# Layer ends of a four-layer block on one core: closing and opening in four and four pieces by token halves, with parts made ahead in idle buffers

## The reference

```python
def reference(x, ...):
    # layer 0: stick-breaking attention and a grouped state-space mixer
    h = rms_norm(x, g);  proj = h @ even_w_in          # 1024 x 5120
    x = x + concat([o_a, o_b]) @ even_w_out            # 1536 x 1024
    # layer 1: gated linear attention
    h = rms_norm(x, g);  proj = h @ odd_w_in           # 1024 x 3088
    x = x + (o * silu(z)) @ odd_w_out                  # 1024 x 1024
    # layers 2, 3: dilated window attention and retention
    for l in range(2):
        shift, scale, gate = split(silu(c) @ w_ada[l] + b_ada[l], 3)
        h = rmsnorm(x, norm_w[l]) * (1 + scale) + shift
        proj = h @ w_in[l]                             # 1024 x 11776
        merged = sigmoid(ga) * (y_att @ w_proj_attn[l]) + sigmoid(gr) * (y_ret @ w_proj_ret[l])
        x = x + gate * (merged @ w_out[l])
    return rmsnorm(x, final_norm_w)
```

## Time and profile before

| | |
|---|---|
| median of 3 runs | 1069.9 us (1068.21 to 1071.53) |
| the profiled execution | 1071.09 us |
| its span from first to last instruction | 1069.3 us |
| mean granted clock of TensorE | 0.986 |
| busy: TensorE, VectorE, ScalarE, GpSimd | 1019.7, 709.5, 566.0, 201.0 us |
| loads: read from HBM | 189.59 MB |

### The profile page before, as it was taken

The page is one execution under the profiler, slowest core; times in us unless marked ns, Lnnn a source line. Parts: engine busy times, 40 slices in busy tenths (PEclk is TensorE's granted clock), DMA queues, the critical chain, the costliest instruction groups (busy, mean ns, idle before and its releaser), DMA issues.

```text
span 1069.3 us, 15213 instructions
## 1 busy us (share of the span) xinstructions
PE 1019.7 (95%) x6020; PEld 894.4 (84%) x6020; DVE 709.5 (66%) x1111; ACT 566.0 (53%) x873; POOL 201.0 (19%) x212
## 2 busy tenths in 40 slices
PE   5899999979999899999999999989999999999995
PEld 5688889868977679998899888867999888998884
DVE  7884946988868656775566586664444555767666
ACT  6969567647435655445553344555444555334552
POOL 4700070433421100000004100020465000320001
PEclk9999999999999999999999999989999999999998
DMA  7543443958754658874466455545777446645551
GB/s 241 158 128 91 144 128 103 321 180 276 249 175 148 202 177 296 301 249 118 138 183 176 155 155 181 178 136 163 235 237 223 119 118 179 187 146 153 183 177 59
DMA packets 93046, 191.62 MB, mean 179 GB/s; under 512 B 6272, under 2 KB 9600, under 8 KB 92976
## 3 DMA queue, kind: packets, MB, share of 16 engines
q1 hardware_dynamic: 88560, 177.30, 53.7%
q0 software_dynamic: 3264, 10.65, 3.0%
q10 hardware_dynamic: 1152, 2.72, 0.7%
HBM read 189.59 MB, written 1.05 MB: 178 GB/s over the span
## 4 chain that ended last, share of the span: by engine, by line
PE 86%; DVE 8%; ACT 4%; issue 1%; DMA 1%; DVEq 0%; ACTq 0%
PE G L598 15%; PE G L600 14%; PE G L599 14%; PE G L607 8%; PE G L610 8%; PE G L609 8%; DVE WL L1521 2%; PE B L561 2%; ACT AR L1040 1%; ACT WH L1040 1%; DVE AR L1911 1%; PE G L636 1%; PE G L638 1%; PE G L637 1%; PE B L900 1%
## 5 line engine op out<-in xcount | busy, mean ns | idle before, releaser
L1521 DVE TENSOR_TENSOR WL<-RAW,WH 128x1024 fp32r<-128x1024 f32 (+2 forms) x306 | 383.3, 1255 | 251.7 <-ACT WH L1040 250.6
L1040 ACT ACTIVATE WH<-RAW 128x1024 fp32r<-128x1024 f32 (+2 forms) x306 | 320.2, 1049 | 282.5 <-PE G L600 144.9
L598 PE MATMUL G<-WH,HTh 128*128 128x512 f32 (+1 forms) x564 | 230.0, 408 | 7.3 <-DVE WL L1521 6.9
L607 PE MATMUL G<-HTh,WH 128*128 128x256 f32 x768 | 219.3, 286 | 0.5 <-DVE HTl L1597 0.5
L600 PE MATMUL G<-WL,HTh 128*128 128x512 f32 (+1 forms) x564 | 219.7, 389 | 0.0
L599 PE MATMUL G<-WH,HTl 128*128 128x512 f32 (+1 forms) x564 | 219.0, 388 | 0.0
L609 PE MATMUL G<-HTl,WH 128*128 128x256 f32 x768 | 217.8, 284 | 0.0
L610 PE MATMUL G<-HTh,WL 128*128 128x256 f32 x768 | 217.7, 283 | 0.0
L607 PEld LDWEIGHTS G<-HTh,WH 128*128 128x128 f32 x768 | 147.6, 192 | 1.9 <-issue 1.7
L609 PEld LDWEIGHTS G<-HTl,WH 128*128 128x128 f32 x768 | 147.6, 192 | 0.4 <-issue 0.2
L610 PEld LDWEIGHTS G<-HTh,WL 128*128 128x128 f32 x768 | 147.5, 192 | 0.0
(11 more groups left out here) (343 smaller groups left out, 1325.4 us busy)
## 6 DMA issues: line engine op xcount, KB each, us to landing
RAW<-in_w_in SPq DMA_DIRECT2D x176, 512.0 KB, 3.8
RAW<-in_even_w_in SPq DMA_DIRECT2D x40, 512.0 KB, 3.6
AR<-in_w_ada_t SPq DMA_DIRECT2D x32, 512.0 KB, 4.8
AR<-in_w_ada_g POOLq DMA_DIRECT2D x32, 256.0 KB, 4.0
RAW<-in_odd_w_in SPq DMA_DIRECT2D x16, 512.0 KB, 4.3
RAW<-in_w_proj_ret SPq DMA_DIRECT2D x16, 512.0 KB, 3.6
RAW<-in_w_out SPq DMA_DIRECT2D x16, 512.0 KB, 3.5
RAW<-in_even_w_out SPq DMA_DIRECT2D x12, 512.0 KB, 4.6
```

What stands on the lines that cost most here:

```text
L598: nc.tensor.matmul(o, xh, wh, start=begins, stop=False)
L607: nc.tensor.matmul(o, fh, h_[:, kx, :], start=begins and f % 2 == 0, stop=False, skip_group_check=True)
L1040: return nc.scalar.activation(out_, ps, ACT.Copy, **kw)
L1521: vt(wl, raw, wh.bitcast(F32), ALU.subtract).then_inc(*dve.mark(LO, n))
```

## The change

The closing has four pieces (CLOSE), the former lone piece among them, and the opening four (OPEN), each by token halves. The last half of a closing is run after the first eight transposes of the opening. Of each layer end six pieces (the closing's last three, the opening's first three) are not split into the rings but into places of the arena `AR` that are free by then (STAND; `ARR` is the same memory in the rounded type); the table `made` queues two splits each at times 2c - 5, 2c - 3 and 2c - 1, where c is the closing's first piece, and none in the six odd times after. ScalarE waits, before it splits into the arena, for the transposes and products that read those places. `next_layer` gets a new order on both engines, with the splits of the opening's third, fourth and fifth piece in it (fourth and fifth in the ring). The root loses two of its small steps: its first guess comes straight from -v/2. ScalarE scales columns 512 to 1023 in place of GpSimd, in the start too; in layers 2 and 3 VectorE makes the affine step of quarters 2 and 3. GpSimd's load of the reset mask moves behind the next load and waits for the opening's third piece. In the last layer only the closing's last three pieces stand in the arena.

```diff
 AHEAD = 2
+CLOSE, OPEN = 4, 4
 EPS = 1e-6
 NEG = -1e30
 MAGIC = 1597463007.0
+MAGIC_H = MAGIC - 2.0 ** 30 - 2.0 ** 22
 RND = 12582912.0
 C1 = 6.28125
...
@@ -321 @@
             v = w.rearrange("(c p) n -> p c n", p=P)
             groups["close", l] = dict(into=into, at=len(pieces), n=512)
-            for j, k in ((0, ks[1]), (1, ks[0]), (1, ks[1])):
+            for j, k in ((0, ks[0]), (0, ks[1]), (1, ks[0]), (1, ks[1])):
                 pieces.append(dict(src=v[:, k:k + KP, 512 * j:512 * j + 512], n=512, kind="C", group=("close", l), k=k,
                                    lhs=lhs, into=into[j], first=False, last=False, split=len(pieces) - groups["close", l]["at"]))
         def opening(name):
-            for i in range(3):
+            for i in range(OPEN):
                 pieces[groups[name]["at"] + i]["split"] = i
...
@@ -402 @@
         s_raw = [sem(f"raw{i}") for i in range(NRAW)]
         HI, LO = events("hi", range(NP)), events("lo", range(NP))
+        STAND = [[(9216, 10240), (11264, 12288)] + [(16896 + 2048 * i, 17920 + 2048 * i) for i in range(4)],
+                 [(4352, 5376), (6400, 7424)] + [(11776 + 2048 * i, 12800 + 2048 * i) for i in range(3)] + [(9728, 10752)],
+                 [(13568, 23424), (14592, 15616), (16640, 17664)] + [(7424 + 2048 * i, 8448 + 2048 * i) for i in range(3)],
+                 [(7424 + 2048 * i, 8448 + 2048 * i) for i in range(3)]]
+        held = {groups["close", l]["at"] + 1 + i: at for l, layer in enumerate(STAND) for i, at in enumerate(layer)}
+        ring = [n for n in range(NP) if n not in held]
+        slot = {n: i % NHL for i, n in enumerate(ring)}
+        before = {n: ring[i - NHL] for i, n in enumerate(ring) if i >= NHL}
+
+        def parts(n):
+
+            if n in held:
+                return tuple(ARR[:, at:at + KP * 512] for at in held[n])
+            return WH[:, slot[n], :], WL[:, slot[n], :]
+
         def w_in(n):
             w = KP * pieces[n]["n"]
-            return RAW[:, n % NRAW, 0:w], WH[:, n % NHL, 0:w], WL[:, n % NHL, 0:w]
+            return (RAW[:, n % NRAW, 0:w],) + tuple(x[:, 0:w] for x in parts(n))
+
+        made = {2 * n - 1: [n + AHEAD] for n in range(1, NP - AHEAD)}
+        for l in range(3):
+            c0 = groups["close", l]["at"]
+            made[2 * c0 - 5], made[2 * c0 - 3], made[2 * c0 - 1] = ([c0 + 2 * i, c0 + 2 * i + 1] for i in range(3))
+            for i in range(6):
+                made[2 * (c0 + i) + 1] = []
...
@@ -578 @@
                 p = pieces[n]
                 if p["split"] is not None:
                     h = 2 * p["split"] + kk
-                    split_half(n - p["split"] + h % 3, h // 3)
+                    split_half(n - p["split"] + h % 4, h // 4)
                     return
...
@@ -622 @@
                 if ti == 0:
                     pe.wait_ge(*LO.of(n))
                 w = p["n"]
+                ends = (1, CLOSE - 1) if p["kind"] == "C" else (OPEN - 1,)
                 o = G[p["into"][ti]][:, 0:w]
                 for c in range(KP):
                     k = p["k"] + c
@@ -631 @@
                             pe.wait_ge(*x)
                     else:
                         pe.wait_ge(*HT_LO.of(layer_of(p["group"]), ti, k // 2))
-                    wh, wl = (x[:, n % NHL, c * w:(c + 1) * w] for x in (WH, WL))
+                    wh, wl = (x[:, c * w:(c + 1) * w] for x in parts(n))
                     xh, xl = (x[:, kx, 128 * ti:128 * ti + 128] for x in (h_, l_))
                     nc.tensor.matmul(o, xh, wh, start=p["first"] and c == 0, stop=False)
                     nc.tensor.matmul(o, xl, wh, start=False, stop=False)
-                    ins = nc.tensor.matmul(o, xh, wl, start=False,
-                                           stop=p["kind"] == "C" and p["split"] in (0, 2) and c == 1)
+                    ins = nc.tensor.matmul(o, xh, wl, start=False, stop=p["split"] in ends and c == 1)
                 if ti == 1:
                     ins.then_inc(*pe.mark(STREAM, "piece", n))
-                elif p["kind"] == "C" and p["split"] != 1:
-                    ins.then_inc(*pe.mark(STREAM, "bank", p["group"], p["split"] // 2))
+                elif p["split"] in ends:
+                    ins.then_inc(*pe.mark(STREAM, "bank", p["group"],
+                                          *((p["split"] // 2,) if p["kind"] == "C" else ())))
...
@@ -703 @@
                 for q in range(2):
                     norm_turn(l, 0, q)
-                for i in range(6):
+                half(first - 1)
+                for i in range(2 * OPEN):
                     half(first + i)
-                    if i in (1, 2):
-                        norm_turn(l, 1, i - 1)
+                    if i in (OPEN - 2, OPEN - 1):
+                        norm_turn(l, 1, i - OPEN + 2)
...
@@ -1058 @@
                 copy(dst[:, c, :], ps[:, 0, :], scale=scale(0))
                 copy(dst[:, c + 1, :], ps[:, 1, :], scale=scale(1)).then_inc(*act.mark(YT_HI, *name))
+            def scaled(l, ti):
+
+                act.wait_ge(*RSTD.of(l, ti))
+                copy(HN[:, ti, 512:1024], X[:, ti, 512:1024], scale=NR[l][:, ti:ti + 1]).then_inc(
+                    *act.mark(HN_A, l, ti))
+
             def turned(l, ti, r):
-                act.wait_ge(*side("nt", l, ti, r // 2))
                 ps = bank_of["nt", l, ti, r // 2]
                 rows = slice(128 * ti, 128 * ti + 128)
-                for k in (2 * r, 2 * r + 1):
-                    j = k % 4
-                    if l < 2:
-                        ins = copy(HTh[:, k, rows], ps[:, 128 * j:128 * j + 128],
-                                   scale=co[("even_g", "odd_g")[l]][:, k:k + 1])
-                    else:
-                        act.wait_ge(*MOD.of(l - 2, "c"))
-                        ins = nc.scalar.activation(HN32[:, k, rows], ps[:, 128 * j:128 * j + 128], ACT.Identity,
-                                                   scale=Acols[l - 2][:, k:k + 1], bias=Bcols[l - 2][:, k:k + 1])
-                if l >= 2:
-                    ins.then_inc(*act.mark(HN_B, l, ti, r))
-                    act.wait_ge(*HN_B.of(l, ti, r))
+                if l > 1 and r > 1:
+                    act.wait_ge(*HN_D.of(l, ti, r))
+                else:
+                    act.wait_ge(*side("nt", l, ti, r // 2))
+                    for k in (2 * r, 2 * r + 1):
+                        j = k % 4
+                        if l < 2:
+                            ins = copy(HTh[:, k, rows], ps[:, 128 * j:128 * j + 128],
+                                       scale=co[("even_g", "odd_g")[l]][:, k:k + 1])
+                        else:
+                            act.wait_ge(*MOD.of(l - 2, "c"))
+                            ins = nc.scalar.activation(HN32[:, k, rows], ps[:, 128 * j:128 * j + 128], ACT.Identity,
+                                                       scale=Acols[l - 2][:, k:k + 1], bias=Bcols[l - 2][:, k:k + 1])
+                    if l > 1:
+                        ins.then_inc(*act.mark(HN_B, l, ti, r))
+                        act.wait_ge(*HN_B.of(l, ti, r))
+                if l > 1:
                     c = slice(2 * r, 2 * r + 2)
                     ins = copy(HTh[:, c, rows], HN32[:, c, rows])
                 ins.then_inc(*act.mark(HT_HI, l, ti, r))
@@ -1094 @@
             def next_layer(l):
                 n0 = (0, 54, H0[0], H0[1])[l]
+                hi(n0 + 2)
+                hi(n0 + 3)
                 square(l - 1, 0, 0)
                 square(l - 1, 0, 1)
-                hi(n0)
-                square(l - 1, 1, 0)
-                hi(n0 + 1)
+                hi(n0 + 4)
+                scaled(l, 0)
                 turned(l, 0, 0)
+                if l > 1:
+                    square(l - 1, 1, 0)
+                turned(l, 0, 1)
+                if l < 2:
+                    square(l - 1, 1, 0)
                 square(l - 1, 1, 1)
-                turned(l, 0, 1)
-                hi(n0 + 2)
                 turned(l, 0, 2)
                 turned(l, 0, 3)
+                scaled(l, 1)
                 for r in range(4):
...
@@ -1555 @@
                 k = slice(ti, ti + 1)
                 y = NR[l][:, k]
-                i, h, z, e, v = (x[:, k] for x in (rs_i, rs_h, rs_z, rs_e, rs_v))
+                h, z, e = (x[:, k] for x in (rs_h, rs_z, rs_e))
                 inv = 1.0 / 1024
                 if l == 0:
                     dve.wait_ge(*SUMSQ.of(0, ti))
-                    ts(v, NSS[0][:, k], inv, EPS, ALU.mult, ALU.add).then_inc(*dve.tick())
+                    ts(h, NSS[0][:, k], -0.5 * inv, -0.5 * EPS, ALU.mult, ALU.add).then_inc(*dve.tick())
                 else:
                     dve.wait_ge(*SUMSQ.of(l, ti, 0))
-                    ts(e, NSS[l][:, k], inv, EPS, ALU.mult, ALU.add).then_inc(*dve.tick())
+                    ts(e, NSS[l][:, k], -0.5 * inv, -0.5 * EPS, ALU.mult, ALU.add).then_inc(*dve.tick())
                     dve.wait_ge(*dve.prev)
```

(62 more changed lines are left out.)

101 lines of the change are left out of this document (59 added, 42 removed).

## The result

The changed kernel takes **1077.5 us** (median of 4 runs, 1076.7 to 1078.2) against 1070.3 for the kernel before in the same comparison: ratio 1.0068, 95% interval 1.0053 to 1.0084. It is slower by 7.2 us, where +3.4 was forecast; the interval lies wholly above 1. The profiled execution took 1076.7 us with a span of 1074.9; before, the span was 1069.3.

The account below looks back on a forecast made before the run. TensorE, 86% of the chain, was taken to bound the kernel, so only its idle or slow-clock time counts. Terms 0.6 + 3.0 + 0.5 - 0.4 - 0.3 = +3.4 on 1069.9 gave 1073.3 us; own range 1070 to 1077, outer 1063.5 to 1078.

Parts of the forecast that it names:

- the second end: Second layer end: waits of 6.1 us against 5.28, less 0.3, so +0.5 us (bounds -0.4, +1.7).
- First waits: TensorE's transposes waiting for scaled rows at the three layer ends: 3.9, 3.3 and 2.0 us forecast.
- second transposes: Transposes of token half 1 at the layer ends, late because the second root follows low parts: about 1.5 to 2 us.
- Denser splits meet GpSimd: Rival: extra low parts slowed beside GpSimd's additions, +1.4, and two more clock falls, +3.4: 1078.1 us; chance 0.17.
- the first end: First layer end: waits of 8.15 us against 4.9, less 0.3, so +3.0 us (bounds +1.5, +5).
- the landing of the fourth piece's load: Opening's ring piece: landing 3.7 to 5.1 us after issue at the second end, 3.3 to 4.0 at the first.
- the 0.3 of cover: Layer ends: 0.3 us taken off each sum for TensorE work the steps leave out, covering part of the waits.
- The third end: Third layer end: waits of 5.5 us against 5.6, less 0.3, so -0.4 us (bounds -1.5, +1).
- The start: Kernel's start: two new ScalarE scalings delay the low parts before TensorE's first matmul, +0.6 us (bounds 0, +1.2).
- The kernel's end: Kernel's end: the root loses 0.2 us and its start 0.1, so -0.3 us.
- The clock: TensorE's falls to half clock around the layer ends: 0, with 1.7 us either way for a fall more or less.
- VectorE keeps up: Rival: the load lands early enough at the layer ends, first waits vanish, one clock fall fewer: 1061.9 us; chance 0.23.

Follow-up runs that it names:

- masks_later: The changed kernel with GpSimd's two small loads at the first end moved behind the wait its third load already has: 1077.1 us, ratio 1.0066.
- norm_alone: The kernel before, with only the short root and the second half of the columns scaled on ScalarE instead of GpSimd: 1075.7 us, ratio 1.0058.
- norm_behind: norm_alone with ScalarE's scalings later, the first directly ahead of the first transposed half, the second behind token half 0: 1068.8 us, ratio 0.9983.
- late splits: The changed kernel with the splits of the opening's fourth and fifth pieces queued later at each layer end: 1062.7 us, ratio 0.9935.

## Why the prediction was right, and which term was mis-sized

**The mechanism.** "VectorE idle before the ring piece's low part with ScalarE's split as releaser and that one idle for its load" is what the trace shows, at the second end with 4.79 and 5.93 us. First waits at all three ends are the longest; the opening's first half waits 0; second transposes are late by 1.72, 0.99 and 0.98 us where 2.1, 1.55 and 1.5 were forecast. The sign and the place were right, the second transposes 0.4 to 0.6 us better than forecast at every end.

**The size** was not: +7.2 us by the medians and +5.6 in the profiled execution for +3.4. 1077.5 us lies 0.5 above the forecast's own range (to 1077) and inside the outer one (to 1078) by the room that was left for a rival. It is nearer to the rival *Denser splits meet GpSimd* (1078.1) than to the forecast (1073.3), though that rival's mechanism is not what the trace shows. Place by place the errors were +2.6 us at the first end, +0.5 before the second, +1.7 at the second and -3.4 at the third: that they cancel in part is luck.

**The term that was too small: the landing of the fourth piece's load.** Second end: 3.7 to 5.1 us assumed, 8.79 measured. The earlier trace rows showed 8.0 as the longest of that stretch, and the prediction named ScalarE's three loads, yet took the median. The first wait became 6.7 us for 3.3; waits of that end sum to 7.7 against 5.3, +2.4, where +0.8 stood before the 0.3 of cover was taken off. The other three waits there came to 1.0 us and not the 2.8 laid out: the opening's first half and the third half, 0.5 and 0.75 late in the forecast, were on time behind the longer first wait. Moving those three loads away cut landing and wait by the same 3.8 us: the runs show this term directly. First end: issue forecast at 224.1 to 225.4 and landing 3.3 to 4.0 us later, measured 226.4 and 6.2; wait 5.7 for 3.9, and the four waits sum to 8.8 for 8.15. So the waits there were nearly the forecast's; of the 2.6 us that this end cost beyond it, 1.6 is the stretch at half clock from 216.3. The issue was late because the whole trace ran 0.9 us behind by then and because the dot product took 2.32 us at 223.66, beside GpSimd's addition from 222.75 to 224.89, where 1.63 was assumed; it took 1.27 us in the trace with the dot's load moved.

**The rival that denser splits meet GpSimd** was half true: in this trace its place was the dot product, not the splits. The three low parts before it took 3.90 us, 1.3 each, under the 1.57 of the earlier trace rows, and the load's issue came 1 us late. In masks_later GpSimd's addition fell beside the last of the same three low parts, which took 4.99 us, and the dot product took 1.27. The collision moved to whoever stood beside the addition. The rule that the Trainium skill has on this (SBUF — State Buffer, section "SBUF: two separate sides"), named in the prediction, fits: the addition ran for another 1.23 us when the dot product began, and the dot product took 1.05 us longer. The rival's two further falls of the clock did come, one each at the first two ends, but as many went elsewhere.

**The third end** came out better: 4.0 us of waits, not 5.5, and 3.8 us given back instead of 0.4 (1.7 of waits, about 1.7 of the clock). The first wait was longer than forecast (2.6 for 2.0), but the opening's waits were 0 and 0.4, the second transposes 1.0, and one of two falls of the clock was gone.

**The start.** +0.6 forecast, +0.9 measured, but hardly by the step that was named: the first product begins at 16.57 us instead of 16.36, +0.2. (The prediction named a time before 16.5 as the sign that this term is wrong; it came just past it.) The rest is the clock: matmuls start 0.21 us apart until 21.7 us and 0.12 apart from then on, where before the change that step came at 18.7. Two kernels with the same start, norm_alone and norm_behind, make it at 16.0 and 20.7 us, and stand 0.4 and 1.2 us behind the kernel before at 30 us, so a term of that size can't be read from one trace. The same holds for a fall of the clock near 50 to 70 us, which comes or goes between kernels that are alike up to there, 1.6 us each time.

**The kernel's end.** -0.3 forecast, +0.2 measured. The last scaling waits for the load of the final norm's weights, which landed 3.7 us after its issue and not 3.3: VectorE stood 1.25 us for it, 0.58 before. The shorter root only made that wait longer.

**The clock** was put at 0, and came to -1.2 us in sum (busy time; 23.9 us at 0.50 in both). It hid two movements: a fall more before the first end and longer ones around the two long waits, against fewer elsewhere. That it could go to 6.8 us once no end waits long was not foreseen. The rival "VectorE keeps up" at 1061.9 us is close to what the late splits give, 1062.7, but by luck: it had 6.6 us from waits and 1.7 from the clock, and against the kernel before the late splits have 2.5 us less idle time and 6.5 us less busy time.

## What to carry to other kernels

In these traces each engine works through its instructions in written order: VectorE's residual stood behind a low part that waited 4.79 us. So a step that isn't needed yet must not stand ahead of the chain that the next stage waits for, unless all that it waits for is there; making work ahead pays where it follows the chain. Three pairs of kernels with the same operations in another order showed it here, for a load, a scalar result and a matmul: 14.8, 7.0 and 2.4 us. The first is the clear one; the second came mostly through the clock, and the third, which moved several steps at once, is within the overlap of its intervals. To price a wait on a load, list what every queue has in flight at its issue. The longest landing of that stretch in the trace before was the better guess here than the median, and still short: 8.0 us for 8.8 at the second end, 5.3 for 6.2 at the first.
